# Ends of two attentions given quarters of the next job, and the last two norm products of the third put side by side

## The reference, cut to what matters

```python
u = rmsnorm(h, mix_pre_g[l])
qa, ka, va, qb, kb, vb, qc, kc, vc, gl = jnp.split(u @ w_in[l], split_at, axis=-1)
oa = neighbourhood_attention(...)           # A: 8 heads, 2D windows, bias table
ob = sliding_window_attention(...)          # B: 8 query heads, 2 key heads, band of 128, rope, sink
oc = differential_attention(...)            # C: 4 pairs of heads, rope, two softmaxes subtracted,
                                            #    then rmsnorm over 128 columns of each head
branches = jnp.stack([oa, ob, oc], axis=2)
yb = jnp.einsum('bsnc,ncd->bsnd', branches, w_branch[l])
gates = jax.nn.sigmoid(gl.reshape(b, s, N_BRANCH, D_MODEL) + b_gate[l])
h = h + rmsnorm(jnp.sum(gates * yb, axis=2) @ w_out[l], mix_post_g[l])
```

## Time and profile before

| | |
|---|---|
| median of 3 runs | 3371.4 us (3369.3 to 3374.7) |
| the profiled execution's own time | 3367.8 us |
| its span, first to last instruction | 3365.9 us |
| PE busy | 3311.3 us, 98% of the span |
| DVE / ACT / POOL busy | 2443.5 / 1688.2 / 849.2 us |
| mean granted TensorE clock | 0.998 |

### The profile page before, as it was taken

How to read it: one execution, slowest core, us unless ns; L and a number is a source line. 1 busy time by engine, 2 the same in 40 slices (tenths; PEclk the granted TensorE clock), 3 DMA queues, 4 the chain that set the end, 5 groups by cost and what they waited for, 6 DMA issues and landing times. The chain is left out here.

```text
span 3365.9 us, 51734 instructions
## 1 busy us (share of the span) xinstructions
PE 3311.3 (98%) x20422; PEld 2948.0 (88%) x20422; DVE 2443.5 (73%) x3936; ACT 1688.2 (50%) x3071; POOL 849.2 (25%) x607
## 2 busy tenths in 40 slices
PE   9999999999999999999999999999999999999998
PEld 7999888888889998999888888899988888888998
DVE  7878765756697769777766666697868676649776
ACT  5445454645455445444554544564547374335543
POOL 3433111021064314432111021063400001206431
PEclk9999999999999999999999999999999999999999
DMA  4333433263223332333423253233322222322332
GB/s 138 107 101 113 115 92 94 62 152 95 82 91 102 109 101 82 101 107 113 118 77 98 70 150 104 67 100 103 114 91 93 86 79 70 107 91 92 98 109 82
DMA packets 118049, 332.79 MB, mean 99 GB/s; under 512 B 18984, under 2 KB 21800, under 8 KB 117808
## 3 DMA queue, kind: packets, MB, share of 16 engines
q1 hardware_dynamic: 105200, 306.30, 29.2%
q0 software_dynamic: 12320, 22.66, 3.4%
q10 hardware_dynamic: 288, 0.52, 0.0%
HBM read 306.23 MB, written 4.21 MB: 92 GB/s over the span
## 5 line engine op out<-in xcount | busy, mean ns | idle before, releaser
L1908 DVE TENSOR_TENSOR wl<-raw,wh 128x1024 fp32r<-128x1024 f32 (+2 forms) x633 | 799.9, 1268 | 276.3 <-ACT wh L1330 269.6
L1330 ACT ACTIVATE wh<-raw 128x1024 fp32r<-128x1024 f32 (+2 forms) x637 | 553.4, 875 | 374.8 <-PE PS L807 354.4
L807 PE MATMUL PS<-bh,wh 128*128 128x256 f32 x2520 | 708.5, 281 | 15.1 <-ACT tmp L1330 8.6
L807 PE MATMUL PS<-bl,wh 128*128 128x256 f32 x2520 | 702.7, 279 | 0.0
L807 PE MATMUL PS<-bh,wl 128*128 128x256 f32 x2520 | 702.5, 279 | 0.0
L807 PE MATMUL PS<-uh,wh 128*128 128x512 f32 (+2 forms) x1656 | 612.8, 370 | 12.8 <-DVE ul L1944 6.4
L807 PE MATMUL PS<-uh,wl 128*128 128x512 f32 (+2 forms) x1656 | 600.0, 362 | 0.0
L807 PE MATMUL PS<-ul,wh 128*128 128x512 f32 (+2 forms) x1656 | 599.6, 362 | 0.0
L807 PEld LDWEIGHTS PS<-bh,wh 128*128 128x128 f32 x2520 | 472.8, 188 | 23.5 <-DVE wl L1908 11.0
L807 PEld LDWEIGHTS PS<-bl,wh 128*128 128x128 f32 x2520 | 473.5, 188 | 0.0
L807 PEld LDWEIGHTS PS<-bh,wl 128*128 128x128 f32 x2520 | 471.9, 187 | 0.4
(11 more groups left out here) (268 smaller groups left out, 5756.2 us busy)
## 6 DMA issues: line engine op xcount, KB each, us to landing
raw<-in_gu SPq DMA_DIRECT2D x218, 512.0 KB, 3.3
raw<-in_win SPq DMA_DIRECT2D x139, 512.0 KB, 3.4
raw<-in_dn SPq DMA_DIRECT2D x80, 320.0 KB, 3.0
raw<-in_dn SPq DMA_DIRECT2D x40, 512.0 KB, 3.7
raw<-in_wbr SPq DMA_DIRECT2D x72, 256.0 KB, 2.7
raw<-in_wout SPq DMA_DIRECT2D x24, 512.0 KB, 3.3
raw<-in_dn SPq DMA_DIRECT2D x40, 256.0 KB, 2.7
raw<-in_wv SPq DMA_DIRECT2D x20, 512.0 KB, 3.3
```

What stands on the lines that cost most here:

```text
L807: return e.matmul(out, lhs, rhs, start=start, stop=stop, skip_group_check=True)
L1330: return e.activation(out, in_, f, scale=scale, **more)
L1908: tt(wl[:, c % 4, 0:n], src, wh[:, c % 4, 0:n], SUB).then_inc(*S.lo.up(("lo", c)))
```

## The change

Five edits, all in stages v = 1 and v = 4:

1. B's steps 32 to 35 each take a quarter of q of A, which stood behind B and now writes bank 0 (the call of `ring(6)` stays, so that later jobs keep their banks).
2. A's steps 32 to 35 each take a quarter of g(0,4), bank 0, which stood ahead of br(0,4). Its piece is now loaded and split ahead of br(0,0)'s. DVE evacuates it where it did, ahead of br(0,4). The gates 5 to 7 and A's branches get banks by hand.
3. C's norm product x = 3 stands right behind the one for x = 2, behind g(1,0); behind g(1,1) there is none.
4. ACT's copy of the turned values stands ahead of its copies for heads 2 and 3 rather than behind that for head 2; DVE's and ACT's steps for head 3 move up behind those for head 2.
5. In B's attention DVE does `stack` ahead of the splits of the same step.

```diff
--- before.py
+++ after.py
@@ -357,7 +357,8 @@
             order = [("q", 1), ("g", 2), ("q", 2), ("g", 3), ("g", 4), ("q", 3), ("g", 5), ("g", 6), ("g", 7)]
             fills[v, "B"] = Fill([gate(1, m, [i % 2]) if a == "g" else proj("B", a, m, 8 + m, [i % 2])
                                   for i, (a, m) in enumerate(order)], [2] * 2 + [1] * 8 + [2, 1] * 4 + [1] * 6 + [0] + [1] * 6 + [0])
-            proj("A", "q", 0, 0, ring(6))
+            proj("A", "q", 0, 0, [0])
+            ring(6)
             proj("A", "k", 0, 4, ring(6))
             values("A", (l, 0))
             for m in range(KT):
@@ -365,10 +366,11 @@
             order = [("k", 1), ("q", 1), ("g", 0), ("k", 2), ("q", 2), ("g", 1), ("k", 3), ("q", 3), ("g", 2), ("g", 3)]
             fills[v, "A"] = Fill([gate(0, m, [i % 2]) if a == "g" else proj("A", a, m, (0 if a == "q" else 4) + m, [i % 2])
                                   for i, (a, m) in enumerate(order)], ([2] * 4 + [1] * 4) * 3 + [1, 0] * 4)
+            gate(0, 4, [0])
             for m in range(KT):
-                if m > 3:
-                    gate(0, m, ring(6))
-                branch(0, m)
+                if m > 4:
+                    gate(0, m, [(1, 3, 5)[m - 5]])
+                branch(0, m, [(1, 2, 3, 4, 5, 2, 4, 0)[m]])
         else:
             proj("S", "k", 0, 4, ring(6, 2))
             proj("S", "q", 0, 0, ring(6))
@@ -702,6 +704,7 @@
 
             return f % 2, 2, 3, 4
 
+        TAIL = {"C": lambda v: ("k", v, "B", 0), "B": lambda v: ("q", v, "A", 0), "A": lambda v: ("g", v, 0, 4)}
         BRANCH = {"C": 2, "B": 1, "A": 0, "S": 0, "F": 1}
         NORMS = [(kind, v) for v in range(6) for kind in ("pre", "post")] + [("pre", 6), ("pre", 7), ("post", 7)]
         INLINE = {("g", v, 0, m) for v in (1, 4) for m in range(4, 8)} | {("g", 6, n, m) for n in (1, 2) for m in range(2, 8)}
@@ -1134,7 +1137,7 @@
                 A = ATT[st]
                 jobs = iter(fill.jobs)
                 now, left = iter(()), [0]
-                tail = dense(JOBS["k", v, "B", 0], v, "u") if st == "C" else iter(())
+                tail = dense(JOBS[TAIL[st](v)], v, "u") if st in TAIL else iter(())
 
                 def filler(steps):
                     nonlocal now
@@ -1165,7 +1168,7 @@
                             scores(v, st, n, b, qs[hh], *ks[hh], S.sc, (st, v, n))
                     if n < len(fill.quota):
                         filler(fill.quota[n])
-                    elif n in (A.n, A.n + 1, A.n + 2, A.n + 4):
+                    elif n in ((A.n, A.n + 1, A.n + 2, A.n + 4) if st == "C" else range(A.n, A.n + 5)):
                         next(tail, None)
                     if st == "S" and n == 1:
                         values_turned(v, "S")
@@ -1242,7 +1245,7 @@
 
             def merge(v, n, m):
                 tag = ("g", v, n, m)
-                if tag in INLINE:
+                if tag in INLINE and (v == 6 or m > 4):
                     run(JOBS[tag], v)
                 run(JOBS["br", v, n, m], v, "o")
 
@@ -1252,19 +1255,19 @@
                 values(v, "C")
                 attention(v, "C", FILLS[v, "C"])
                 late = [JOBS["q", v, "B", 0], JOBS["t", v, "B"], JOBS["g", v, 1, 0], JOBS["g", v, 1, 1]]
-                for x in range(4):
-                    run(late[x], v)
-                    if x == 2:
+                for n in range(4):
+                    run(late[n], v)
+                    if n == 2:
                         values_turned(v, "B")
-                    b = 6 + (x + 1) % 2
-                    take(b, S.dv, "c_n", v, x)
-                    E.wait_ge(S.dv, "c_diag", v, x)
-                    i = mm(bank(b), ones[:, :], tmp[:, x % 2, X0:TW], True, True)
-                    i.then_inc(*S.st.up(("c_n", v, x)))
+                    for x in ((0,), (1,), (2, 3), ())[n]:
+                        b = 6 + (x + 1) % 2
+                        take(b, S.dv, "c_n", v, x)
+                        E.wait_ge(S.dv, "c_diag", v, x)
+                        i = mm(bank(b), ones[:, :], tmp[:, x % 2, X0:TW], True, True)
+                        i.then_inc(*S.st.up(("c_n", v, x)))
                 for m in range(KT):
                     merge(v, 2, m)
                 attention(v, "B", FILLS[v, "B"])
-                run(JOBS["q", v, "A", 0], v)
                 run(JOBS["k", v, "A", 0], v)
                 values(v, "A")
                 for m in range(KT):
@@ -1766,10 +1769,12 @@
                         stack(("k", v, "B", 0))
                     if x == 2:
                         stack(("q", v, "B", 0))
-                    E.wait_ge(S.dv, "c_n", v, x)
-                    act(obh[:, x, :], GB[4 + x][:, X0:TW], ACT.Copy).then_inc(*S.an.up(("c_oh", v, x)))
                     if x == 2:
                         values_turned(v, "B", (S.pv, "C", v, 15))
+                    for y in ((0,), (1,), (2, 3), ())[x]:
+                        E.wait_ge(S.dv, "c_n", v, y)
+                        act(obh[:, y, :], GB[4 + y][:, X0:TW], ACT.Copy).then_inc(*S.an.up(("c_oh", v, y)))
+                    if x == 2:
                         tanh(v, 1, 0)
                 tanh(v, 1, 1)
                 for m in range(KT):
@@ -2480,10 +2485,13 @@
                             gated(job)
                         else:
                             evacuate(job, v, len(job.chunks) - 1)
-                    ahead(fill_reach(fill, n))
+                    if st != "B":
+                        ahead(fill_reach(fill, n))
                     for job in fill.ended(n - A.wait):
                         if job.kind in "qk":
                             stack(job.tag)
+                    if st == "B":
+                        ahead(fill_reach(fill, n))
 
             def gated(job):
 
@@ -2573,11 +2581,12 @@
                         evacuate(JOBS[late[x]], v)
                     if x == 2:
                         stack(q)
-                    scale(x)
-                    if x < 2:
-                        diagonal(x + 2)
-                    if x:
-                        low_c(x - 1)
+                    for y in ((0,), (1,), (2, 3), ())[x]:
+                        scale(y)
+                        if y < 2:
+                            diagonal(y + 2)
+                        if y:
+                            low_c(y - 1)
                 low_c(3)
                 for m in range(KT):
                     merge(v, 2, m)
```

## The result

The changed kernel has a median of 3365.07 us over 20 executions (3360.1 to 3370.4), the kernel before 3371.35 us over 20 (3365.0 to 3374.7). The ratio is 0.9984, with a 95% interval of 0.9978 to 0.9990. By the ratio that is 5.4 us less (3.4 to 7.4; the medians themselves lie 6.3 apart): a small gain, within the 0.2% that I called no change. The forecast was 3365.5. The profiled execution took 3365.05 us, with a span of 3363.2 us, 2.7 us less than before, where the sum of the prediction was 5.9.

A forecast was written before the change was run, and what follows sets the result against it. PE, busy 98%, was taken to bound the kernel. Terms -3.5 + 1.0 - 2.2 - 1.2 = -5.9 us gave 3361.9 from the profiled 3367.8, and 3365.5 from the median 3371.4; range 3360.4 to 3369.4.

The forecast's parts named there:

- end of A: At A's end, quarters of g(0,4) fill PE's wait for ACT's copy: -1.75 us in each stage, -3.5 in all.
- end of B: At B's end, q of A waits for bank 0: new wait 2.4 us, old wait 2.0, +1.0 us in all.
- stacks: In B's step 6, stacking ahead of the split removes the scores' wait: -2.2 us (bounds -1.0 and -2.3).
- norm products: Behind C, a 0.8 us wait at bank 6 replaces the branches' wait for `obl`: -0.6 us each, -1.2 in all.
- start of A: The larger waits at A's start (2.86 us in stage 1) hang on a late load and stay.
- clock: The sum counts no clock fall: around A's start PE stopped for 2.86 us and the clock stayed at 1.00.
- Rival (d): Behind A's five branches, gates g(0,5) to g(0,7) come late: sum +11.3 us, 3382.7 us; chance 0.06.
- Rival (a): At B's end bank 0 doesn't bind and B gains as A does: -10.5 us, 3360.9 us; chance 0.12.
- rival (b): Small waits at scores and `obl` only move; A and B alone count: -2.5 us, 3368.9 us; chance 0.17.
- rival (c): The clock falls at B's longer stop, 1.7 us lost twice: -2.5 us, 3368.9 us; chance 0.07.
- main case: The summed forecast for the whole kernel: -5.9 us, 3365.5 us, own bounds 3362.8 to 3367.5; chance 0.58.

The follow-up runs named there:

- e3: The kernel before with only the edit at A's end, g(0,4) in quarters over A's steps 32 to 35: 3364.23 us, ratio 0.9982 to the kernel before.
- e1: The changed kernel with q of A at B's end writing bank 1 instead of bank 0: 3359.21 us, ratio 0.9968 to the kernel before.
- e9: The changed kernel with B's four quarters of q of A one step later, steps 33 to 36, bank 0: 3361.22 us, ratio 0.9976 to the kernel before.
- e4: The kernel before with only B's stacks put ahead of the splits: 3365.54 us, ratio 0.9992 to the kernel before.
- e6: The changed kernel with head 3's norm product in bank 5 instead of bank 6: 3365.06 us, ratio 0.9987 to the kernel before.
- e7: The changed kernel with banks 0 and 1 exchanged for A's filler jobs, later banks matched: 3360.42 us, ratio 0.9971 to the kernel before.

## Why the prediction was right, point by point

| term | predicted us | measured in the trace us |
|---|---|---|
| end of A | -3.5 | -3.51 (1.76 and 1.75 gone, nothing new) |
| end of B | +1.0 | +1.16 (2 x 2.41 for 1.73 + 1.93) |
| stacks | -2.2 | -2.9 (1.23 and 1.04 gone, 0.26 twice at the second stack, slower restarts) |
| norm products | -1.2 | -1.3 (waits: 1.31 + 1.00 to 0.73 + 0.56; 0.3 of slower restarts) |
| start of A | 0 | -0.03 (3.01 + 1.47 to 2.03 + 2.42) |
| clock | 0 | +3.4 in this profile, some +2 in the mean |
| sum | -5.9 | -3.2 in this profile (the stretches: -3.6; the span: -2.7), -4.6 with the mean |

**End of A**: right in size and mechanism; e3 shows it alone. Rival (d), gates late behind the five branches, did not come up in any kernel with this edit.

**End of B**: right. The bank binds until the evacuation of g(1,7), shown by e1 (other bank: stop gone) and by e9 (work ahead of it: stop shorter by that work, same end). Rival (a) is what e1 made of it: its price of 4.6 us below the forecast compares with 4.82 us of waits.

**Stacks**: right, and none of it returned (e4). The sum left out a second stack of B that scores waited for, 0.26 us a stage; I had read only the larger waits of the earlier trace rows. **Norm products**: right in size and mechanism; the wait for bank 6 came as predicted, 0.57 idle instead of 0.8, and `obl` was on time by 0.3 us. Half of rival (b) is thus refuted by the profile; the chain that it feared is there, though, and e6 shows it as soon as PE comes 0.7 us earlier. The price of 0.86 us a product stands too, alone and two in a row (e6).

**The clock**: this is the step that failed, as a matter of degree. I gave rival (c) 0.07 and the main case the clock of 1.00, because around A's start PE had stopped for 2.86 us without a fall. One profile of before was too little for that. In the profiles of the other kernels ten of fourteen stops of 2.0 us or more at these two places were followed by a fall. In the changed kernel it gave back some 2 us in the mean, so that the result lies between the main case and (c): -6.6 by the waits, about -4.6 with the falls; the interval of the measured -5.4 (-3.4 to -7.4) holds both. That 3365.5 and 3365.07 agree to half a microsecond is therefore partly luck: an uncounted gain of 0.8 (the second stack, and the restarts behind the waits) and an uncounted loss of some 2 stand against each other, within what the times can tell.

The Trainium skill, "TensorE: Matmul & The Clock Gate", section "HAM oscillation — how this bites in real kernels", has a matmul engine that was left waiting, there some 3 to 5 us for a DMA, begin its next burst cold. Here, with shorter stops, this held for 4 of 6 of 2.41 us and for 0 of 18 of 1.64 to 1.93 us, so it deserved a higher chance than I gave it.

**Start of A**: "hangs on a late load and stays" was right for the sum, but the reason was incomplete. That PE waits there at all comes from the bank, as e7 shows: in its profile ACT waits 2.90 us for a load at this place, and PE goes on. That the load decides how long the wait for the bank is, 1.0 to 3.1 us, is my reading; no run isolates it.

## What to carry to other kernels

Work moved into a gap fills it only if its output bank is free there: look up who held the bank last and when that is read. Here a bank number made the difference between a loss of 1.2 us and a gain of 3.7. Where a bank must stay, put the work behind what can run without it: the wait is shorter by that work, and here no fall of the clock followed the shorter stop (e9: 1.64 us for 2.41). And before a small wait is taken away, ask what the same chain needs next: the norm product's bank and the `obl` behind it were one wait, not two.

## What the runs showed of the hardware

- A granted clock of about 0.5 for 3.41 us at a time, 1.6 to 1.7 us lost each, was seen behind ten of fifteen stops of PE of 2.03 us and more at the two places above. Why one stop of 2.41 us is followed by it and the next is not stays open. Length alone does not decide either: in stage 6 one of 1.61 us was followed by a fall in 11 of 12 profiles; there PE had been busy for only 1.06 of 3.00 us.
- The spread of the executions goes with the mean granted clock. In 63 executions of the kernel before, the mean time is 3367.6 us at a mean clock of 0.998, 3371.0 at 0.997 and 3374.3 at 0.996 (29, 23 and 6 of them): some 3.4 us a step, as two falls would cost. The other 5, at 0.999, took 3367.2, only 0.4 less. At equal mean clock the changed kernel is 5.7 us faster, between the 5.4 of the ratio and the 6.6 of the waits.
- An fp32 matmul of 512 columns costs 0.86 us. Its two records begin 0.43 us apart, and what is left of it shows at the next dense matmul (0.63 us from start to start instead of 0.23). Two in a row take 1.72 us.
- At A's scores PE started 0.09 us after the last landing of the DMAs it had waited for, five times out of five.
